# Two-layer hybrid trunk on one core: the first output unit of block 0 by tile pairs, and the load of the next x behind the third sum

## What is computed

```python
def even_layer(x, norm_g, w_in, conv_w, pool_w, pool_scale, w_out):
    h = rmsnorm(x, norm_g)
    xa, bg, cg, gate_a, u, gate_b = split_cols(h @ w_in, EVEN_SIZES)
    ya = short_conv_mixer(xa, bg, cg, conv_w) * jax.nn.silu(gate_a)
    yb = pool_mixer(u, pool_w, pool_scale) * jax.nn.silu(gate_b)
    return x + jnp.concatenate([ya, yb], axis=-1) @ w_out
...
def odd_layer(x, norm_g, w_in, i_bias, f_bias, sinks, w_out):
    ...
    yd = (mem * jax.nn.sigmoid(do.astype(jnp.float32))).astype(x.dtype) * jax.nn.silu(gate_d)
    return x + jnp.concatenate([yc, yd], axis=-1) @ w_out
```

## Time and profile before

| | |
|---|---|
| median of 3 runs | 1625.11 us (1623.35 to 1626.89) |
| profiled execution, its own time | 1624.13 us |
| its span (first to last instruction) | 1622.3 us |
| PE busy | 1605.9 us, 99% of the span |
| DVE, ACT, POOL busy | 953.4, 506.7, 499.5 us |
| DMA over the span | 404.97 MB, 250 GB/s |
| granted TensorE clock, mean | 0.998 |

### The profile page before, as it was taken

One profiled execution on the slowest core, in us unless ns is written; L12 is line 12 of the kernel. 1 busy time (PEld: TensorE's weight loads), 2 busy tenths in 40 slices (PEclk: granted clock), 3 DMA queues, 4 the chain that ended last, 5 costly groups with the idle time before them and its releaser, 6 DMA issues.

```text
span 1622.3 us, 21426 instructions
## 1 busy us (share of the span) xinstructions
PE 1605.9 (99%) x7977; PEld 1329.3 (82%) x7977; DVE 953.4 (59%) x1636; ACT 506.7 (31%) x1251; POOL 499.5 (31%) x570
## 2 busy tenths in 40 slices
PE   8999999999999999999999999999999999999998
PEld 7887788888888878888788887888878888788887
DVE  4857336685443872778652275367784237446767
ACT  4011224553200133455420022445441012243643
POOL 8777675568345313333340001000043000100001
PEclk9999999999999999999999999999999999999999
DMA  9987689668888877776895576653498558664448
GB/s 314 329 285 265 215 286 292 198 215 294 298 286 306 322 291 256 249 264 205 343 326 191 193 253 264 217 166 138 143 381 298 193 191 298 241 206 137 143 168 324
DMA packets 182815, 404.97 MB, mean 250 GB/s; under 512 B 33156, under 2 KB 84888, under 8 KB 182712
## 3 DMA queue, kind: packets, MB, share of 16 engines
q1 hardware_dynamic: 162400, 379.38, 67.0%
q10 hardware_dynamic: 20312, 24.24, 4.8%
HBM read 309.12 MB, written 94.44 MB: 249 GB/s over the span
## 4 chain that ended last, share of the span: by engine, by line
PE 93%; DVE 3%; DMA 2%; ACT 1%; issue 0%; SPq 0%; ACTq 0%; POOLq 0%; POOL 0%; DVEq 0%
PE bank L823 14%; PE bank L825 14%; PE bank L824 14%; PE pair_a L823 5%; PE pair_a L825 5%; PE pair_a L824 5%; PE pair_b L823 5%; PE pair_c L823 5%; PE pair_b L825 4%; PE pair_b L824 4%; PE pair_c L825 4%; PE pair_c L824 4%; PE pair_a L1235 2%; PE pair_b L1205 1%; PE pair_b L1206 1%; PE pair_c L1137 1%
## 5 line engine op out<-in xcount | busy, mean ns | idle before, releaser
L823 PE MATMUL bank<-h_hi,slot 128*128 128x512 f32 (+1 forms) x976 | 378.8, 388 | 1.7 <-DVE h_lo L1850 1.0
L825 PE MATMUL bank<-h_hi,slot 128*128 128x512 f32 (+1 forms) x976 | 377.7, 387 | 0.0
L824 PE MATMUL bank<-h_lo,slot 128*128 128x512 f32 (+1 forms) x976 | 377.6, 387 | 0.0
L823 PEld LDWEIGHTS bank<-h_hi,slot 128*128 128x128 f32 x976 | 184.0, 189 | 38.8 <-DVE h_lo L1850 1.3
L825 PEld LDWEIGHTS bank<-h_hi,slot 128*128 128x128 f32 x976 | 184.0, 189 | 37.3
L824 PEld LDWEIGHTS bank<-h_lo,slot 128*128 128x128 f32 x976 | 184.1, 189 | 35.9
L673 POOL TENSOR_TENSOR slot<-stages,slot 128x512 fp32r<-128x512 f32 x132 | 180.2, 1365 | 11.0
L644 POOL TENSOR_TENSOR rs<-sums,small 128x1 f32<-128x1 f32 x43 | 15.2, 353 | 539.0 <-ACT proj L1397 325.4
L671 POOL TENSOR_SCALAR slot<-stages 128x512 fp32r<-128x512 f32 x132 | 96.2, 729 | 101.1 <-issue 97.1
L823 PE MATMUL pair_a<-h_hi,slot 128*128 128x512 f32 x256 | 100.3, 392 | 0.0
L825 PE MATMUL pair_a<-h_hi,slot 128*128 128x512 f32 x256 | 99.7, 390 | 0.0
(11 more groups left out here) (488 smaller groups left out, 3425.8 us busy)
## 6 DMA issues: line engine op xcount, KB each, us to landing
slot<-split_weights SPq DMA_DIRECT2D x356, 512.0 KB, 4.3
split_weights<-slot SPq DMA_DIRECT2D x132, 512.0 KB, 4.4
slot<-combined_weights SPq DMA_DIRECT2D x76, 512.0 KB, 5.2
stages<-in_even_w_in SPq DMA_DIRECT2D x48, 256.0 KB, 3.9
stages<-in_odd_w_in SPq DMA_DIRECT2D x36, 256.0 KB, 3.6
stages<-in_even_w_out SPq DMA_DIRECT2D x32, 256.0 KB, 4.3
combined_weights<-keys SPq DMA_DIRECT2D x16, 512.0 KB, 4.2
combined_weights<-stages SPq DMA_DIRECT2D x32, 256.0 KB, 3.0
```

The source lines that it names most:

```text
L823: t.matmul(dst, l_hi, r_hi, start=start, stop=False)
L824: t.matmul(dst, l_hi, r_lo, start=False, stop=False)
L825: return t.matmul(dst, l_lo, r_hi, start=False, stop=stop)
```

## The change

Four edits. At the start PE takes the first half of tile 0's transposes ahead of the transpose of the weight rows; ACT's copy of the convolution weights moves from behind tile 0 to behind tile 2, and PE waits for it before it writes `banks[1]`. In block 0's first output unit, tiles 0 and 1 are done with both halves first, then tile 2 with both (behind `pool_u`), then tile 3 with both (behind `pool_gate`), and the fourth group's product comes behind the next pair. In blocks 1 and 2 `load_x` stands behind the third `sum_hi` and no longer ahead of the first.

```diff
-            def raw_transposes(tt):
+            def raw_transposes(tt, halves=(0, 1)):
 
                 pe.wait_ge(s_x[tt], 16)
-                for hb in range(2):
+                for hb in halves:
...
             keep_warm(WARM)
+            raw_transposes(0, (0,))
             pe.wait_ge(s_gain, 16)
             pe.wait_ge(s_const, 16)
             t.transpose(banks[1][:, 0:KT + 12], first_rows, ident[0:KT + 12, 0:KT + 12]).then_inc(s_weight_col, 1)
-            raw_transposes(0)
+            raw_transposes(0, (1,))
             raw_transposes(1)
...
                         for j in range(2):
+                            if j == 1:
+                                pe.wait_ge(s_weight_col, 3)
...
-                    for kk in range(2):
-                        slot(2 * U_EOUT + kk)
-                        for tt in range(TT):
-                            if kk == 0 and tt == 0:
-                                pe.wait_ge(s_pool_gate, b * 4 + 3)
-                            if kk == 0 and tt == 2:
-                                pe.wait_ge(s_pool_gate, b * 4 + 4)
-                            last = token_part(U_EOUT, 0, kk, tt, y_hi, y_lo, 0, True, False)
-                        last.then_inc(s_half, 1)
-                    pool_product(3)
+                    for kk, tt in ((0, 0), (0, 1), (1, 0), (1, 1), (0, 2), (1, 2), (0, 3), (1, 3)):
+                        if tt == 0:
+                            slot(2 * U_EOUT + kk)
+                        if (kk, tt) == (0, 0):
+                            pe.wait_ge(s_pool_gate, b * 4 + 3)
+                        if (kk, tt) == (0, 2):
+                            pe.wait_ge(s_pool_u, b * 4 + 4)
+                        if (kk, tt) == (0, 3):
+                            pe.wait_ge(s_pool_gate, b * 4 + 4)
+                        last = token_part(U_EOUT, 0, kk, tt, y_hi, y_lo, 0, True, False)
+                        if tt == TT - 1:
+                            last.then_inc(s_half, 1)
                     for kp in (1, 2, 3):
                         if kp >= 2:
                             pe.wait_ge(s_ye, b * 8 + 2 * kp + 2)
                         token(U_EOUT + kp, kp, y_hi, y_lo, 0, False, kp == 3)
+                        if kp == 1:
+                            pool_product(3)
...
                 evacuate_raw(tt)
-                if tt == 0:
+                if tt == 2:
                     a.activation(conv_w[:, :, :].rearrange("p k c -> p (k c)"), banks[1][:, KT:KT + 12], ACT.Copy).then_inc(s_weight_col, 1)
...
-                load_x(b, (0, 1))
                 act.wait_ge(s_att_out, b * 8 + 8)
                 sum_hi(ODD_SUM1)
                 sum_hi(ODD_SUM2)
                 sum_hi(ODD_SUM3)
+                load_x(b, (0, 1))
                 sum_hi(ODD_SUM4)
```

## The result

| | before | after |
|---|---|---|
| median | 1623.89 us (21 runs, 1622.64 to 1628.25) | 1626.14 us (21 runs, 1621.51 to 1631.38) |
| profiled execution | 1624.13 us | 1628.1 us |
| its span | 1622.3 us | 1626.3 us |
| granted clock, mean | 0.998 | 0.996 |

The ratio after to before is 1.0015, 95% interval 1.0008 to 1.0022. The medians are 2.25 us apart, where +2.5 was forecast. The change is slightly slower, by less than the 0.2% that the chances went by, but not by nothing: the interval leaves out 1.

What follows compares the result with a forecast made beforehand. The prediction took PE, busy 99% of the span, as the bound. Its terms -0.3 - 1.9 + 1.8 + 2.9 gave +2.5 us on a median of 1625.1, so 1627.6 us, range 1622.0 to 1630.0.

Steps and rivals of the forecast that it cites:

- The start, -0.3: Start: ACT begins tile 0 earlier and the first matmul moves with it; -0.3 us, ends 0 and -0.4.
- if the rise keeps its instant, work that begins 0.4 us earlier is done at half speed: Start: first matmuls run at 1.2 GHz until the clock rises, so 0.4 us earlier gives only 0.2.
- Block 0's unit, -1.9: Block 0's first output unit: PE's 1.86 us lost to `pool_gate` goes; -1.9 us, ends -1.7 and -1.9.
- the cover of the wait for `pool_gate` and that of kp = 3: Block 0: the gate is ready 0.9 us before PE asks, the fourth group's last y_lo 2.4 us before.
- The load of x, +1.8 and +2.9: Ends of blocks 1 and 2: late x delays ACT, then DVE, then PE's next transposes; +1.8 and +2.9 us.
- with the same lag it lands at 794.78 + 9.7 = 804.5: Block 1: x's second transfer keeps its 9.7 us from issue to landing, making ACT 4.3 us late.
- first rival, x in time: Blocks 1 and 2: x's lag falls to block 0's 6.2 us; sum -3.7 us, 1621.4 us; chance 0.2.
- The relief of the spares: Block 1: spare loads come sooner, PE reaches the transposes about 1 us earlier but gains nothing, waiting for DVE.
- x behind the weights: Blocks 1 and 2: x's lag is the spare loads' 12.6 us; sum +8.2 us, 1633.3 us; chance 0.08.
- The clock that stays up behind 11 us: Start: less PE idle, so the clock may not fall; 1.7 us gained, 1625.9 us; chance 0.12.
- The pair kp = 3: Block 0: stretched DVE casts make this pair wait, giving back the unit's gain; 1629.5 us; chance 0.02.

Runs made afterwards that it cites:

- start_alone: The kernel before with the edits at the start alone; 1622.27 us, ratio 0.9989 to before.
- x_late_alone: The kernel before with only the load of x moved behind the third sum; 1628.6 us, ratio 1.0028 to before.
- unit_alone: The kernel before with only block 0's first output unit reordered and its fourth product later; 1622.56 us, ratio 0.9994 to before.
- filled_wait: The changed kernel with 18 useless 256-column matmuls in PE's wait ahead of L837's first transposes, blocks 1 and 2; 1624.95 us, ratio 1.0003 to before.
- ab_x_early: The changed kernel with the load of x put back ahead of the first sum; 1621.21 us, ratio 0.9975 to before.
- after_again: The changed kernel, unchanged, profiled a second time; 1628.72 us.
- copies_first: The changed kernel with ACT's two copies of Q1's banks ahead of its squares of x; 1620.83 us, ratio 0.9974 to before.
- x_behind_second: The changed kernel with the load of x behind the second sum, not the third; 1620.31 us, ratio 0.9975 to before.
- second_copies_first: The changed kernel with x loaded behind the second sum and Q1's copies ahead of x's squares; 1621.84 us, ratio 0.998 to before.
- start_filled: x_behind_second with six more useless identity products at the start; 1619.77 us, ratio 0.9983 to before.
- before_again: The kernel before, unchanged, profiled a second time; 1622.93 us.

## Why the prediction was right, and which terms were mis-sized

**The start, -0.3.** Right in the profile: the first matmul at 11.61 against 11.90, ACT's start 6.14 against 6.38. The step "if the rise keeps its instant, work that begins 0.4 us earlier is done at half speed" fits those traces where the clock fell: the product that marks the end of this stretch (L957, L960 in after) begins at 31.36 before and at 31.12 after, 31.15 in start_alone. The term was sized from one trace only. Where the clock did not fall, the mark is at 30.71 in the second trace of before, at 30.52 in x_late_alone, and at 29.36 to 29.58 in five traces of kernels with the edits. So there the edits are worth about 1.1, and the rows show why: without the edits all eight transposes of tile 0 stood behind the weight rows and ran slowly (1.97 us), ACT began its first copy only at 7.05 and 7.24, and the first matmul at 12.58 and 12.77. With the edits half of them were done before the weight rows came, and the first matmul is at 11.43 to 11.63 whether the transposes ran fast or slowly. The whole of the difference between a fall and none is 0.7 to 1.8. With the gain of 0.3 in some executions and 1.1 in others, start_alone's -1.8 (-3.6 to 0) is no surprise; whether the edits also make the fall rarer is open. It was there in 4 of 9 traces with them and in 2 of 4 without (of all thirteen traces), which tells nothing.

**Block 0's unit, -1.9.** Right, exactly: no bracket, even matmuls, the cover of the wait for `pool_gate` and that of kp = 3 both held. From its first output matmul, before had started the seventh 3.23 us later, at 151.76; after starts its own 1.36 us later. The median of unit_alone shows 1.0 of it (-2.6 to +0.6), which doesn't contradict it and doesn't confirm it.

**The load of x, +1.8 and +2.9.** The mechanism was right at each link. The step that was mis-sized is "with the same lag it lands at 794.78 + 9.7 = 804.5". The lag was 8.8 and 8.6, so 0.9 and 1.2 us less. The distance from the third sum to L837 grew from 16.46 to 17.35 in block 1, +0.9, and from 15.42 to 17.16 in block 2, +1.7: the forecast's terms less those 0.9 and 1.2. (Against the second trace of before, 15.64 and 15.16, the growth is 1.7 and 2.0, so this match rests on the first trace of before.) The text had named a possible reason under its first rival, that SP issues nothing beside x at 794; after's trace shows no issue of SP from 791 to 797 us, and three in the 4.9 us behind that. No run tests it alone, and what came was about 1 us of lag, not the 3.5 that this rival needed. The lag stayed above the 8 us below which the text had called itself wrong, and ACT's square of tile 1 began at 801.91, where it had said 802.3. The relief of the spares came as forecast, and as forecast it gave nothing: PE was done with Q6's last matmul at 808.05, 15.4 us behind the third sum and not 16.5, and then stood for 1.98.

**The term that was missing** is the clock behind those waits: 1.6 and 1.4 us in after's trace, shown apart from the wait by filled_wait. The forecast had looked for the clock at the start only, where it was already low, and priced a wait of PE at its length. In the profiled execution the sum is -0.3 - 1.9 + 0.9 + 1.7 + 1.6 + 1.4 = +3.4, and the measured one is +4.0; the rest lies between the places and is within what two traces of before differ by (1.2 us). So the forecast of +2.5 came close because two errors of opposite sign nearly met: 2.1 us too much for the waits, 3.0 too little for the clock. The medians say the same of the luck and share it out otherwise: the edits at the start and in block 0 gained 4.1 and not 2.2, the move of x cost 6.5 and not 4.7 (x_late_alone has 4.5 for it), and the difference is +2.4. By either reckoning the sign and the path were foreseen, and the closeness of the number was luck.

**The spread.** After's runs reach from 1621.5 to 1631.4, before's from 1622.6 to 1628.3. The granted clock of each run goes with it: after's four runs at a mean clock of 0.996 average 1629.4 us, its two at 1.000 average 1623.0. Sixteen of its 21 runs are at 0.998 or less; in filled_wait and ab_x_early, where PE does not stand idle there, it is 3 of 12 each. But x_late_alone, which has the same two waits, has 5 of 12, and 8 of the 35 runs of before beside it, so this count points to the waits and doesn't prove them.

**The rivals.** x in time needed a lag of 6.2, x behind the weights one of 12.6; neither came near. The clock that stays up behind 11 us did come, in after_again, though with slow transposes before it, and after's total was no lower for it (1628.72). The pair kp = 3 did not give the gain back.

**A better version.** ab_x_early, copies_first and x_behind_second (0.9974 to 0.9975) beat both kernels; second_copies_first (0.998) and start_filled (0.9983) can't be told from them. x_behind_second is the least of an edit: the same change, with the load one sum earlier.

## What to carry to other kernels

When a transfer is moved later, write down every instruction that its first consumer's engine has queued behind that consumer, and the time at which each is wanted; the price is read there (here two copies behind two squares), and moving these ahead of the wait (copies_first) is as good as issuing earlier (x_behind_second). Take the lag from the same transfer in the same loaded stretch, and keep 1 us of room on it, since it moved by that here when the transfer was issued 8 us later. A wait on TensorE of 2 us in an otherwise full stretch is to be priced at its length plus the slow stretch that may follow it, here 1.5 us more.

## What the runs showed of the hardware that was not expected

The granted clock fell to 0.50 for about 3.4 us behind waits of PE of 2.0 to 2.5 us, in five of six such waits in blocks 1 and 2 (after, after_again, x_late_alone); it cost 1.4 to 1.6 us each time. It did not fall there in any of the traces in which PE waited 0.4 us or less or did useless products meanwhile. How it is decided whether it falls can't be told from these traces: the one that did not was 2.13 us long, and one of 1.98 us did. Elsewhere in the program the length of a wait decides as little. Behind the 1.7 us wait on block 0's gate product the clock stayed at 1.00 in all four traces that have it (before, before_again, start_alone, x_late_alone). Behind copies_first's 2.14 us in block 0 it was low for 6.8 us. And x_behind_second lost it for 3.4 us behind waits of 0.78 and 1.08 us, 2 us apart, which second_copies_first has too (0.92 and 1.08) without a fall:

```profile
749.00:750.00 1.00, 1.00 (x4) 0.75 (x3) 0.97 (x2) 0.52 (x1) 0.71 (x1) 0.50 0.00 0
```

The second of two x transfers of 512 KB took 8.6 to 9.1 us from issue to landing when asked for behind the second or third sum, and 9.4 to 10.5 when asked for ahead of the first, where SP was issuing weight loads beside it; in block 0, with little else loading, 6.2. By the Trainium skill, "DMA: Bandwidth & Descriptors", section "Anatomy of one DMA — SWDGE (gpsimd) path", which the forecast had cited, a transfer takes about 2.0 us plus its bytes over 436 GB/s, which makes an estimate of 4.4 us for both tiles. The page gives that fit for transfers issued by GpSimd, and these go from ACT's queue. The first of the two took 6.5 to 8.4 us in blocks 1 and 2 and the second 8.6 to 10.5, so on a loaded chip the rows decide.
